# Attention's row maximum and the convolution's tiles between DVE, POOL and ACT, in one decoder layer

## The reference, cut to what matters

```python
logits = (jnp.einsum('bthd,btkhd->bthk', q, kg).astype(jnp.float32) * (HEAD_DIM ** -0.5)
          + bias.astype(jnp.float32))
logits = jnp.where((rel >= 0)[:, :, None, :], logits, NEG_INF)
p = jax.nn.softmax(logits, axis=-1).astype(vg.dtype)
...
c = jax.nn.silu(layernorm(causal_dwconv(u_ext, lw['conv_dw'], lw['conv_db']),
                          lw['conv_ln_g'], lw['conv_ln_b']))
x = x + jnp.concatenate([a, c], axis=-1) @ lw['w_o']
```

## Time and profile before

| | us |
|---|---|
| median of 3 runs (lowest, highest) | 1980.56 (1979.04, 1982.94) |
| the profiled execution | 1980.32 |
| its span, first to last instruction | 1978.3 |
| PE busy in the span | 1705.3 (86%) |
| DVE busy | 1223.9 (62%) |
| POOL busy | 754.5 (38%) |
| ACT busy | 548.9 (28%) |

### The profile page before, as it was taken

One profiled execution on the slowest core, in us unless ns is written; L12 is line 12 of the kernel. 1 busy time (PEld: TensorE's weight loads), 2 busy tenths in 40 slices (PEclk: granted clock), 3 DMA queues, 4 the chain that ended last, 5 costly groups with the idle time before them and its releaser, 6 DMA issues.

```text
span 1978.3 us, 27650 instructions
## 1 busy us (share of the span) xinstructions
PE 1705.3 (86%) x10197; PEld 1550.4 (78%) x10197; DVE 1223.9 (62%) x1961; ACT 548.9 (28%) x1112; POOL 754.5 (38%) x401
## 2 busy tenths in 40 slices
PE   4389999996886778959968869999999999999983
PEld 3388899992653456739967759999999999999973
DVE  1454699999986998843363274545445454545456
ACT  4234621211221443431134133231122113212312
POOL 0412133328993397602300114354344434443420
PEclk9789999995877998979978679999999999999987
DMA  6301112211624000031101201111111111111102
GB/s 247 88 17 48 44 53 74 66 43 45 186 68 130 1 1 1 1 118 32 32 11 38 80 22 54 43 44 50 48 43 53 42 42 53 42 49 46 42 15 90
DMA packets 128845, 109.09 MB, mean 55 GB/s; under 512 B 10772, under 2 KB 110348, under 8 KB 128354
## 3 DMA queue, kind: packets, MB, share of 16 engines
q1 hardware_dynamic: 118597, 101.19, 16.7%
q10 hardware_dynamic: 10157, 6.67, 1.1%
HBM read 92.49 MB, written 16.00 MB: 55 GB/s over the span
## 4 chain that ended last, share of the span: by engine, by line
PE 74%; DVE 14%; ACT 4%; issue 4%; DMA 2%; SPq 1%; POOL 1%; ACTq 0%; DVEq 0%; POOLq 0%
PE ps L1571 54%; PE ps L1563 4%; DVE conv_sum L1348 4%; PE ps L1588 4%; PE ps L1804 2%; PE ps L1855 2%; PE ps L1826 1%; DVE n_rstd L1153 1%; DVE n_rstd L1158 1%; PE ps L1778 1%; DVE logits L1404 1%; PE ps L1759 1%; PE ps L1746 1%; PE ps L1671 1%; DVE logits L1407 1%
## 5 line engine op out<-in xcount | busy, mean ns | idle before, releaser
L1571 PE MATMUL ps<-h_hi,w_hi 128*128 128x344 f32 (+1 forms) x1752 | 563.9, 322 | 27.4 <-DVE h_lo L1377 21.8
L1571 PE MATMUL ps<-h_lo,w_hi 128*128 128x344 f32 (+1 forms) x1752 | 561.6, 321 | 0.0
L1571 PE MATMUL ps<-h_hi,w_lo 128*128 128x344 f32 (+1 forms) x1752 | 561.4, 320 | 0.0
L656 POOL TENSOR_SCALAR w_hi<-w_raw 128x1024 fp32r<-128x1024 f32 (+1 forms) x107 | 116.3, 1087 | 960.7 <-PE ps L1571 710.2
L1571 PEld LDWEIGHTS ps<-h_hi,w_hi 128*128 128x128 f32 (+1 forms) x1752 | 329.6, 188 | 31.2 <-issue 22.3
L1571 PEld LDWEIGHTS ps<-h_lo,w_hi 128*128 128x128 f32 (+1 forms) x1752 | 329.7, 188 | 2.4
L1571 PEld LDWEIGHTS ps<-h_hi,w_lo 128*128 128x128 f32 (+1 forms) x1752 | 329.9, 188 | 0.4
L658 POOL TENSOR_TENSOR w_lo<-w_raw,w_hi 128x1024 fp32r<-128x1024 f32 (+1 forms) x107 | 286.9, 2681 | 8.9
L1533 DVE TENSOR_TENSOR xT<-xT,ps 128x344 f32<-128x344 f32 x264 | 135.3, 513 | 173.1 <-PE ps L1571 172.3
L1514 DVE SCALAR_TENSOR_TENSOR up_conv<-up,fw,up_conv 128x1024 f32<-128x1024 f32 x44 | 61.9, 1406 | 197.4 <-ACT upl L1108 197.4
L1571 PE MATMUL ps<-g_hi,w_hi 128*128 128x344 f32 x528 | 169.3, 321 | 9.5 <-POOL g_lo L749 8.6
(11 more groups left out here) (326 smaller groups left out, 2740.0 us busy)
## 6 DMA issues: line engine op xcount, KB each, us to landing
w_raw<-in_w_up SPq DMA_DIRECT2D x44, 512.0 KB, 3.8
w_raw<-in_w_in SPq DMA_DIRECT2D x24, 512.0 KB, 3.8
w_raw<-in_w_down SPq DMA_DIRECT2D x22, 512.0 KB, 3.7
s_k_page<-in_cache_k SPq DMA_DIRECT2D x32, 256.0 KB, 2.9
s_v_pages<-in_cache_v SPq DMA_DIRECT2D x32, 256.0 KB, 3.0
x_spill<-xT SPq DMA_DIRECT2D x1, 4128.0 KB, 12.5
xT<-x_spill SPq DMA_DIRECT2D x1, 4128.0 KB, 13.7
x_tok<-in_x_prompt SPq DMA_DIRECT2D x2, 2048.0 KB
```

Of the source, the lines that this page charges most:

```text
L656: pool.tensor_scalar(view(wh), view(wr), 1.0, 0.0, ALU.mult, ALU.add).then_inc(w_hi, 1)
L1571: mm = pe.matmul(out, view(w)[:, k, m0:m0 + m], x(k), start=(k == 0 and q == 0), stop=(k == ktiles - 1 and q == 2))
```

## The change

Two things.

The first is the maximum. The additions scale by -1/8 and keep a minimum, so that their by-product is the negated scaled maximum that the exponential wants. From block 2 on the far addition starts its minimum from the near one's result, so it waits for it (`self_.link`). The small operation L1413 goes, ACT waits for `added`, and the exponential's scale is -1.

The second is who convolves. DVE keeps tile 0 alone, a tap at every even item. POOL makes tiles 1, 2 and 3: 93 steps, 40 of them ahead of the attention, and 3 or 4 after each near addition. Tiles 1 and 2 are made as before. For tile 3 POOL makes only the first product and the sums. The 30 other products are made by ACT, in turn in two buffers, one of them POOL's scratch tile: one at each item from 38 on, two at items 39, 47, 55 and 63, between the exponential and what follows it. ACT waits until the sum two products back has been made (`px_used`; the first count is POOL's last step of tile 2), POOL until the product is there (`px_ok`).

```diff
-POOL_FIRST = 36
-POOL_AFTER_NB = {2: 1, 3: 1, 4: 2, 5: 2, 6: 3, 7: 4}
+POOL_FIRST = 40
+POOL_AFTER_NB = {2: 3, 3: 4, 4: 4, 5: 4, 6: 4, 7: 4}
+PX_FIRST = 38
...
-    yt1 = r.take("conv_sum1", [P, S])
+    pxs = [r.take("conv_product_a", [P, S]), yx]
...
         def tap_step(n):
 
-            m, n = (2, n) if n < CW else (3, n - CW)
+            m, n = 1 + n // CW, n % CW
...
+            if m == 3:
+                pool.wait_ge(px_ok, n)
+                px = pxs[(n - 1) % 2]
+                if j:
+                    self_.link(pool.tensor_tensor(yp[:, :], yp[:, :], px[:, :], ALU.add))
+                    pool.sem_inc(px_used, 1)
+                else:
+                    pool.tensor_tensor(y[:, m, 0:S], yp[:, :], px[:, :], ALU.add).then_inc(p_conv, 1)
+                return
...
+                self_.link(pool.tensor_tensor(y[:, m, 0:w], yp[:, 0:w], yx[:, 0:w], ALU.add))
                 if m == 2:
-                    self_.link(ins)
-                else:
-                    ins.then_inc(p_conv, 1)
+                    pool.sem_inc(px_used, 1)
...
-        for n in range(n, 2 * CW):
+        for n in range(n, 3 * CW):
             tap_step(n)
...
+        def product():
+
+            nonlocal n_px
+            if n_px:
+                act.wait_ge(px_used, n_px)
+            n_px += 1
+            j = HALO - n_px
+            act.activation(pxs[(n_px - 1) % 2][:, :], u[:, 3, j:j + S], ACT.Copy, scale=cw[:, CT * j + 3:CT * j + 4]).then_inc(px_ok, 1)
...
-                act.wait_ge(mx_ok, i + 1)
+                act.wait_ge(added, i + 1)
                 if h == 0 and b >= 2:
                     act.wait_ge(nrm, b - 1)
-                act.activation(row, row, ACT.Exp, bias=mx[:, i % 4, 2:3], scale=DH ** -0.5,
+                act.activation(row, row, ACT.Exp, bias=mx[:, i % 4, 2:3], scale=-1.0,
                                accum_out=rs[:, b % 2, h:h + 1]).then_inc(exp_ok, 1)
+            if PX_FIRST <= i < len(ITEMS):
+                product()
+                if i % NH == 7:
+                    product()
             if i % NH == 2 and 2 <= i // NH + 1 < NB:
                 q_heads(i // NH + 1)
...
-                ins = dve.tensor_tensor_reduce(out=lg[i % 3][:, k0:ext], in0=pair(i)[:, k0:ext], in1=add, scale=1.0, scalar=CAUSAL,
-                                               op0=ALU.add, op1=ALU.max, accum_out=mx[:, i % 4, 0:1])
+                ins = dve.tensor_tensor_reduce(out=lg[i % 3][:, k0:ext], in0=pair(i)[:, k0:ext], in1=add, scale=-DH ** -0.5,
+                                               scalar=-CAUSAL, op0=ALU.add, op1=ALU.min, accum_out=mx[:, i % 4, 0 if b >= 2 else 2:1 if b >= 2 else 3])
                 if b >= 2:
+                    self_.link(ins)
                     ins = dve.tensor_tensor_reduce(out=lg[i % 3][:, 0:k0], in0=pair(i)[:, 0:k0],
-                                                   in1=sc[:, IDX_AT[b]:IDX_AT[b] + k0], scale=1.0, scalar=CAUSAL,
-                                                   op0=ALU.add, op1=ALU.max, accum_out=mx[:, i % 4, 1:2])
+                                                   in1=sc[:, IDX_AT[b]:IDX_AT[b] + k0], scale=-DH ** -0.5, scalar=mx[:, i % 4, 0:1],
+                                                   op0=ALU.add, op1=ALU.min, accum_out=mx[:, i % 4, 2:3])
                 ins.then_inc(added, 1)
-                dve.wait_ge(added, i + 1)
-                far = mx[:, i % 4, 1:2] if b >= 2 else mx[:, i % 4, 0:1]
-                dve.tensor_scalar(mx[:, i % 4, 2:3], mx[:, i % 4, 0:1], far, -DH ** -0.5, ALU.max, ALU.mult).then_inc(mx_ok, 1)
...
-            if i % 2 and i // 2 < CW:
-                tap_of(1, yt1, tap1, i // 2)
```

More of the change, by code:

```diff
@@ L457, in build @@
     y_ok, ln_s, ln_c, ln_sq, ln_ss = (sem(x) for x in ("y_ok", "ln_s", "ln_c", "ln_sq", "ln_ss"))
-    tap0, tap1, nrm, aT_n = sem("tap0"), sem("tap1"), sem("nrm"), sem("aT_n")
+    tap0, px_ok, px_used, nrm, aT_n = (sem(x) for x in ("tap0", "px_ok", "px_used", "nrm", "aT_n"))
     ln_var, ln_rstd, ln_h, ln_act, ln_hi, ln_lo = (sem(x) for x in ("ln_var", "ln_rstd", "ln_h", "ln_act", "ln_hi", "ln_lo"))
@@ L703, in tap_step @@
             else:
-                ins = pool.tensor_tensor(y[:, m, 0:w], yp[:, 0:w], yx[:, 0:w], ALU.add)
+                self_.link(pool.tensor_tensor(y[:, m, 0:w], yp[:, 0:w], yx[:, 0:w], ALU.add))
                 if m == 2:
-                    self_.link(ins)
-                else:
-                    ins.then_inc(p_conv, 1)
+                    pool.sem_inc(px_used, 1)
         for r in range(2):
@@ L994, in q_heads @@
             ins.then_inc(qz_ok, 1)
+        n_px = 0
+        def product():
[5 more added lines that the diff above has]
+            act.activation(pxs[(n_px - 1) % 2][:, :], u[:, 3, j:j + S], ACT.Copy, scale=cw[:, CT * j + 3:CT * j + 4]).then_inc(px_ok, 1)
         act.wait_ge(qz_0, 1)
@@ L1052, in _ @@
             if i < NB:
-                act.wait_ge(mx_ok, N_ITEMS + i + 1)
+                act.wait_ge(mx_ok, i + 1)
                 if i >= 2:
@@ L1353, in layer_norm @@
             dve.wait_ge(tap0, CW)
-            dve.wait_ge(tap1, CW)
             dve.wait_ge(p_conv, 1)
@@ L1866, in _ @@
         pe.wait_ge(tap0, CW)
-        pe.wait_ge(tap1, CW)
         pe.wait_ge(added, N_ITEMS)
```

## The result

The changed kernel takes 1999.45 us at the median of six runs (1993.09 to 2006.84), the kernel before 1980.33 (1978.05 to 1992.75, six runs). The ratio is 1.009 with a 95% interval of 1.0062 to 1.0117: slower by 19 us, where 7 were forecast, and outside the range given. The profiled execution took 1995.16 us with a span of 1993.4, at the low end of its runs. So the two traces show 15.1 us of the difference; the other 4 lie in the scatter of the runs.

What follows compares the result with a forecast made beforehand. DVE was taken to set the pace in block 4 and PE in block 7 of the prompt's attention. +4.1 + 1.0 + 2.1 = +7.2 us gave 1987.5 us; own range 1982 to 1993, overall range 1972 to 1996.

Steps and rivals of the forecast that it cites:

- +4.1 up to item 40: Attention's first part: item 40's exponential starts at 740.0 us, 4.1 us later than before.
- +1.0 to item 63: From item 40's exponential to item 63's: 104.1 us against 103.1 before, +1.0 us.
- +2.1 at the end: At item 63 ACT makes two products before copying item 61, and the next transposes wait: +2.1 us.
- four steps: Ahead of the attention: POOL's four more steps, 14.6 us, fit in its 28.3 us idle time and cost nothing.
- a wait of POOL: POOL up to item 40's near addition: never idle, finishing at 716.6 us without collisions, no wait counted.
- The taps that POOL loses by: Items 0 to 38: each of 20 DVE taps costs POOL 0.87 us, 17.4 us together.
- The hand-over: Item 39: ACT's third product waits for POOL's first tile 3 sum until 738.4; item 40's exponential starts at 740.0 us.
- The loop over two items: Items 40 to 63: ACT's queue with the product sets 3.88, 4.13 and 4.51 us an item in blocks 5, 6, 7.
- one fall of the clock: Items 40 to 63: PE's idling before 740 us makes one item at 1.2 GHz likely, 3.0 us dearer.
- The maximum: Additions in blocks 2 to 7: 0.08 us gained an item, 4 us at 48 items, only where DVE is the bound.
- the clock stays down: Rival, from item 39 on: ACT stalls idle PE, three more clock falls at 3 us each give 1996 us; chance 0.15.

Runs made afterwards that it cites:

- skip_four: The changed kernel with four of POOL's steps ahead of the attention left out (tile 1 lacks four taps): ratio interval 1.0036 to 1.0088.
- copy_first: The changed kernel with ACT's product behind the copy of the transposed probabilities instead of ahead of it: 1982.91 us.
- min_only: The kernel before with the negated scaled minimum alone, the convolution as it was: gains 10 to 12 us.
- min_and_dummy: The kernel before with the minimum, plus a small DVE operation of the old size that nobody waits for: 1985.04 us.

## Why the prediction was wrong

The direction was right, slower, and most of the mechanism. The sum was +7.2 us: +4.1 up to item 40, +1.0 to item 63, +2.1 at the end. The trace has +9.3, +1.4 and +5.3, and -0.9 for the rest. Three terms are off: four steps and a wait of POOL, both put at nothing, and the end, put too low.

**First failed step: "Four more steps (4 x 3.65 = 14.6 us) lie inside that and cost nothing".** I named POOL's own idle time as their cover and never looked at what DVE did in it. DVE was busy with masks, collisions cost it 0.7 to 2.0 us an operation of the last one, and its lead over PE went; the four steps themselves took 20.8 us (592.29 to 613.06). Item 0 comes 1.8 us late though PE's sample sums came 2.1 us earlier (610.04 against 612.19), so the step costs some 4 us in this trace, 4.5 against skip_four's, and some 2 us in the seven others.

**The taps that POOL loses by.** "I take 0.87": products take 1.97 instead of 1.12 us and sums 3.2 instead of 2.35 when they meet a tap, as forecast. The excess of 22 products and 21 sums over those bases is 10.1 + 5.5 = 15.6 us, where 17.4 were forecast. (POOL idled 54.0 of 219 us before, a quarter and not "a third of that time".) One collision, DVE's tap and POOL's product:

```profile
671.88 1.50 DVE L1371 SCALAR_TENSOR_TENSOR conv_sum<-u,cw,conv_sum 128x1024 f32<-128x1024 f32 x1
```

```profile
672.40 1.97 POOL L710 TENSOR_SCALAR conv_product_p<-u,cw 128x1024 f32<-128x1024 f32 x1
```

The tap ends at 673.38, 0.98 us after the product started, and the product loses 0.85 us. The Trainium skill (SBUF — State Buffer, "SBUF: two separate sides") has the later of the two wait until the other ends. This row agrees within 0.13 us, since the wait is what is left of the tap, and not its whole 1.28 us, as the forecast had read the page.

**Second failed step, the largest: "With no collision POOL would finish the one for item 40 at 620.0 + 7 x 2.33 + 22 x 3.65 = 716.6 us".** It has no wait of POOL in it. Near additions are 18.7 us apart from 681.41 on (700.20, 718.81, 737.56), as forecast. But POOL idles 5.60 us at 660.82, until DVE has made the additions of item 19, since the near biases have two buffers. The earlier trace rows had shown this very wait, 54.0 us of it, and the sum left it out. It is there in all eight traces with this table, 5.6 to 7.0 us; no run takes it out alone. So the near biases of item 40 are ready at 739.9 instead of 734: +2.1 for the start, +5.6 for the gate, -1.8 for the collisions. That is 5.9, and the exponential comes 5.1 us after the forecast.

**The hand-over** was right in its chain, with 4.98 us of wait at its head; the runs without it price it at 3.5 us. (Its sum, 734 + 1.2 + 2.44 + 0.87, is 738.5 and not 738.4.)

**The loop over two items** was right: 104.5 us from item 40 to item 63, forecast 104.1. copy_first gives 95.0, so the place of the product costs 9.5 us of these; I had seen it, and priced it, as what eats the gain.

**Third failed step, the end: "the next transposes waited for that copy, so +2.1 us".** The size was off: +5.3. The two products are 2.1 us; the idle time of 2.62 us behind them is followed by half clock, and the transposes of item 62, the product of item 61 with v and the transposes of item 63 take 6.7 us from start to start of what follows (853.59 to 860.33), where copy_first needs 3.5 at full clock: 3.2 us dearer, and 2.1 + 3.2 = 5.3. I had counted one fall of the clock, at item 40, and none here.

**The maximum: "At 48 items that is 4 us, only where DVE is the bound".** The link is as forecast (far starts 0.46 us after near in the changed kernel, 654.08 against 653.62). But blocks 0 and 1 have one addition and no link, and gain the small operation's whole 0.25 us an item; blocks 2 to 7 gain 0.80 - 0.74 = 0.06 us. That corrects the sum to 16 x 0.25 + 48 x 0.06 = 6.9 us; min_only's trace gained 5.0 in the attention. Alone it is worth 10 to 12 us in the medians, in the change 0 to 2, which is not told from nothing. This error was on the other side, and hidden.

Of the rivals, "the clock stays down" gave 1996, nearest to the result, which is luck in the main: it had the right place at the end, but no gate, and falls between where there were none: the clock stood at 1.00 in blocks 6 and 7 of the changed kernel.

## What to carry to other kernels

Work that is not urgent goes behind the copy or hand-over that another engine waits for, not ahead of it on the same queue: here the place alone was worth 14 us. Idle time of one engine is free only if what it does there slows no other engine; look at the other engines' timelines in the same window before booking nothing. A wait that the rows show in the kernel before stays in the sum until something removes it. And an operation of 0.2 us on the engine that sets the pace is worth its time on the queue at every item, while the same edit beside a changed balance is worth nothing: so measure the parts singly.

## What the runs showed of the hardware

- DVE operations beside POOL's on wide tiles lose time too, and not only POOL's: a scan over 1024 columns 4.26 us instead of 2.28, a mask 3.25 instead of 1.23, while POOL's product loses 0.85 us in the attention and up to 1.85 us beside those masks (2.97 instead of 1.12).
- A small DVE operation (128x1) that depends on the addition before it costs the queue 0.25 us: it starts 0.12 us after the accumulator's read before it begins (before and min_and_dummy), and what follows it starts 0.13 us later.
- After idling 2.62 us PE worked at 1.2 GHz until the 24 matmuls and transposes behind it and eight more were done (granted clock 0.50 from 854 to 860 us of the changed kernel); after 0.83 us it stayed at 2.4 GHz (1.00, copy_first).
- The executions of one kernel in one group lie 4 to 21 us apart, with the same code; the part behind the attention alone took 1125.7 us in one execution of the changed kernel and 1131.5 in another.
